# First load in one array, tiled head sums, ScalarE order and grouped state reads in a hybrid RWKV / attention / MoE block

## The chip, the cores and the metric

The kernel runs on one core of a Trainium2 chip. The metric is the device time of one execution in microseconds (us). The core has TensorE (PE in the profile), VectorE (DVE), ScalarE (ACT), GpSimd (POOL) and SyncE (SP, which here only issues DMAs). All arithmetic is float32.

## The reference

One layer on 256 tokens of width 1024: a combined input projection that feeds an RWKV7 group and a differential-attention group, an output projection, cross-attention to 256 memory tokens, and a mixture of 32 experts (top 4 per token). Cut to what matters here:

```python
xn = rms_norm(x, norm1_g); proj = xn @ w_in            # 1024 x 3328
p = p + (token_shift(p) - p) * mu                       # first 1792 columns
r, k, v, wd, ad, gd = split_cols(p, ...)                # r, k, v: 8 heads of 64
kk = (k * k_k).reshape(B, T, H, N)
kk = kk / maximum(sqrt(sum(kk * kk, -1)), 1e-12)        # one factor per head and token
def step(S, inp):                                       # recurrence over tokens
    sa = einsum('bhvk,bhk->bhv', S, -kkt)
    S = S * wt + sa * (kkt * at) + vt * kt
    return S, einsum('bhvk,bhk->bhv', S, rt)
h = x + concat([y_rwkv, y_diff]) @ w_out
h = h + cross_attn(rms_norm(h), rms_norm(mem))
h = h + moe(rms_norm(h))                                # 32 experts, 403 MB of weights
out = rms_norm(h, final_g)
```

## The kernel before

Everything is written out by hand in one function, `program` (L94), with one block per engine; the order in each block is the order in which that engine works, and semaphores are the only ties between them. PSUM has 8 banks. A table (`place`, from L277) gives each product a bank and a turn in it; `begin` makes TensorE wait until the bank's last user has been copied out ("drained"), `product` makes a reader wait until it is filled.

**Weights before the experts.** The projection weights are cut into chunks of 256 columns (1 MB each). SP loads them in the order of `PRE_CHUNKS` (L79) into a ring of three slots, a slot being free once the product that used it is finished. A chunk product on TensorE is 16 matmul calls (2 halves of 128 columns, 8 contraction steps, 256 tokens), each of which is two instructions of a profile row: 32 instructions a chunk. Chunks in2, in3, in6 are multiplied with x times the norm gain only (`gx`), and their products are scaled with the norm factors afterwards, by VectorE (`scale_products`, L1703); the factors come from TensorE (`factors`, L1001) out of a diagonal that VectorE computes from the sums of squares of x (`spread`, L1669). The other chunks use the normalised xT (L1711).

**The start.** SP issues x transposed and chunk in2 in three parts each, alternating (L474, L475), then x in rows (L478, for the sums of squares), then in3, mem, in6, mem transposed (L480 to L484) and small arrays. VectorE writes gx step by step (L1691), TensorE does the first half of in2 over its 8 steps, then the second.

**RWKV group.** ScalarE takes each product times 1 - mu (L704, `unshifted`), VectorE adds the shifted part (L1728, `shift`), which drains the bank. The head norm goes: kk squared (L1742), `ksum` on TensorE (L1033, four accumulating matmuls that sum each head's 64 rows into 8 rows), clamp and reciprocal root on VectorE (8 rows, L1762), `kb` on TensorE (L1059, which spreads the 8 rows back to 128), product on VectorE (L1786). Between ksum and kb stand chunk in1, the four groups of low-rank products (L1046, L1052; ScalarE drains them with L720 and L693) and chunk in4. The chain on VectorE from L1769 to L1810 gives AR and BT (`ab_ready`), from which TensorE forms L (L1079). The inverse of L's diagonal blocks goes out and in over small DMAs that ScalarE's queue issues (L745, L755, L761, L766), the last eight of them (L766) write XTb, which TensorE needs before chunk in11 (L1166). Then come the state matrices of 8 chunks of 32 tokens; `step(c)` (L1247) advances the state, VectorE adds (L1938), `read_state(c)` (L1262) reads it. Quarters of the chunk products kv2 and kv3 (`filler`) are put between the steps. VectorE also does `combine(2)` (L1878 to L1885) in that stretch, for which TensorE waits in `turn_weights(2)` (L995).

**The mem side.** ScalarE sums mem's squares (L679), VectorE makes the factors (L1667 to L1674), TensorE spreads them (L1008) and VectorE scales memT with them (L1682), all before chunk in0 and in1; memT is first used by kv0.

**Experts.** 96 units of 4 MB stream through five places in the chip's memory; a unit's load is issued when TensorE has finished with the one that held its place (L445, L511, L532). The first units are issued while w_out and wq_x are multiplied (L390 to L395).

## Time and profile before

| | us |
|---|---|
| runs of the kernel before: median of 3 (lowest to highest) | 1248.64 (1248.36 to 1252.04) |
| the profiled execution's own time | 1247.27 |
| its span in the profile | 1245.4 |
| PE busy in the span | 1198.3 (96%) |
| PE weight loads / DVE / ACT / POOL busy | 573.0 / 310.5 / 197.1 / 14.4 |
| chain that ended last | PE 71%, DMA 25%, ACT 2%, DVE 1%, issue 1% |
| HBM read | 443.47 MB, mean 357 GB/s |

TensorE's matmuls are pipelined, so a row's duration for one instruction (0.38 us for 256 columns) is longer than its share of a run of them (6.91 us for the 32 instructions of a chunk). The chain of work that ended last shows the second kind of number, which adds up; the timeline shows starts. A row's bracket says how long the engine was idle before it, and what ended that. "issue" is idle time that no semaphore of the profile explains. The granted TensorE clock was 1.00 of full speed in all stretches up to 1120 us and 0.99 in the rest. The first 338 us hold everything before the experts.

### The profile page before, as it was taken

The page shows a single profiled execution, that of the slowest core. Times are in us where ns is not written, and L with a number is a line of the kernel's source. Part 1 is how long each engine was busy: PE and PEld are TensorE (multiplying, and loading weights), DVE is VectorE, ACT ScalarE, POOL GpSimd, SP SyncE. Part 2 cuts the span into 40 slices and gives each one's busy share as a digit, 9 for nine tenths or more (in the row PEclk, how much of TensorE's full clock was granted, in tenths as well). Part 3 has the DMA queues.
Part 4 walks back from the last instruction along what each step waited for, and adds up shares of the span by engine and source line. Part 5 has one row for each costly group of instructions (what it writes and reads, how often), then busy time and mean ns, then how long its engine had stood idle before and what let it go on. Part 6 is the DMA issues. An engine that isn't in the chain of part 4 may idle for free.

```text
span 1245.4 us, 17482 instructions
## 1 busy us (share of the span) xinstructions
PE 1198.3 (96%) x7452; PEld 573.0 (46%) x7452; DVE 310.5 (25%) x771; ACT 197.1 (16%) x371; POOL 14.4 (1%) x56
## 2 busy tenths in 40 slices
PE   7998999999999999999999999989999999999998
PEld 6787878888733333333333333323333333333333
DVE  5774245203411211121121112111112211111212
ACT  2313243011211111111111111111111111111101
POOL 4000000000000000000000000000000000000000
PEclk9999999999999999999999999999999999999999
DMA  9332213937799999999999999999999999999995
GB/s 326 133 119 79 103 70 105 415 156 274 300 383 436 418 410 436 429 430 433 429 431 435 428 434 431 430 434 431 430 434 430 433 433 431 430 434 431 426 426 230
DMA packets 29922, 445.52 MB, mean 358 GB/s; under 512 B 8432, under 2 KB 8816, under 8 KB 11440
## 3 DMA queue, kind: packets, MB, share of 16 engines
q1 hardware_dynamic: 24944, 443.74, 84.8%
q10 hardware_dynamic: 4928, 1.05, 0.4%
q8 instruction: 39, 0.64, 0.2%
q14 instruction: 11, 0.09, 0.0%
HBM read 443.47 MB, written 1.31 MB: 357 GB/s over the span
## 4 chain that ended last, share of the span: by engine, by line
PE 71%; DMA 25%; ACT 2%; DVE 1%; issue 1%; ACTq 0%; SPq 0%; DVEq 0%
PE ps L1519 22%; DMA ring<-in_moe_w 15%; PE ps L1559 14%; PE ps L960 10%; DMA arena<-in_moe_w 9%; PE ps L981 7%; PE ps L1463 4%; PE ps L1437 3%; PE ps L1422 2%; PE ps L1451 1%; ACT arena L908 1%; PE ps L1168 1%; PE ps L1456 1%; PE ps L995 1%; DMA ring<-in_w_in 1%
## 5 line engine op out<-in xcount | busy, mean ns | idle before, releaser
L1519 PE MATMUL ps<-ring,arena 128*64 128x512 f32 x1248 | 273.6, 593 | 13.8 <-DMA ring<-in_moe_w 13.2
L1519 PE MATMUL ps<-arena 128*64 128x512 f32 x792 | 174.0, 593 | 8.5 <-DMA arena<-in_moe_w 8.5
L1519 PEld LDWEIGHTS ps<-ring,arena 128*64 128x64 f32 x1248 | 88.9, 137 | 194.2 <-issue 173.2
L1559 PE MATMUL ps<-ring,arena 128*64 128x512 f32 x576 | 127.7, 595 | 0.0
L900 ACT ACTIVATE arena<-arena 128x512 f32<-128x512 f32 x31 | 19.5, 629 | 678.8 <-DVE arena L2119 678.8
L2119 DVE TENSOR_SCALAR arena<-ps 128x512 f32<-128x512 f32 x31 | 21.4, 691 | 397.3 <-PE ps L1519 397.3
L960 PE MATMUL ps<-arena,ring 128*128 128x256 f32 x480 | 107.9, 385 | 8.0 <-DMA ring<-in_w_in 8.0
L1519 PEld LDWEIGHTS ps<-arena 128*64 128x64 f32 x792 | 56.4, 137 | 123.4 <-issue 109.6
L960 PEld LDWEIGHTS ps<-arena,ring 128*128 128x128 f32 x480 | 91.4, 192 | 22.0 <-issue 7.9
L1559 PE MATMUL ps<-arena 128*64 128x512 f32 x408 | 90.7, 595 | 0.4 <-DMA arena<-in_moe_w 0.4
L2132 DVE COPY arena<-ps 128x512 f32<-128x512 f32 x32 | 22.1, 692 | 234.9 <-PE ps L1559 234.9
L1559 PEld LDWEIGHTS ps<-ring,arena 128*64 128x64 f32 x576 | 39.8, 137 | 86.6 <-issue 86.6
L1463 PE MATMUL ps<-arena,rws 64*128 64x512 f32 x256 | 63.6, 615 | 0.2 <-DVE arena L2132 0.2
L1437 PE MATMUL ps<-arena 128*64 128x512 f32 x248 | 60.1, 605 | 0.0
L1559 PEld LDWEIGHTS ps<-arena 128*64 128x64 f32 x408 | 28.2, 137 | 61.6 <-issue 60.3
L2100 DVE TENSOR_TENSOR arena<-ps,prm 128x512 f32<-128x512 f32 x32 | 22.1, 691 | 87.7 <-PE ps L1451 85.5
L981 PE MATMUL ps<-ring,arena 128*128 128x256 f32 x192 | 42.6, 381 | 0.0
L1463 PEld LDWEIGHTS ps<-arena,rws 64*128 64x128 f32 x256 | 22.0, 186 | 40.7 <-issue 40.2
L693 ACT ACTIVATE arena<-ps 128x512 f32<-128x512 f32 (+1 forms) x39 | 21.9, 574 | 118.2 <-PE ps L960 52.3
L900 ACT ACT_TABLE_LOAD x31 | 39.8, 1283 | 1.3 <-issue 0.7
L981 PEld LDWEIGHTS ps<-ring,arena 128*128 128x128 f32 x192 | 36.2, 190 | 5.2 <-issue 0.4
L1422 PE MATMUL ps<-arena 32*64 32x512 f32 x264 | 35.9, 613 | 0.0
(308 smaller groups left out, 866.2 us busy)
## 6 DMA issues: line engine op xcount, KB each, us to landing
ring<-in_moe_w SPq DMA_DIRECT2D x51, 4096.0 KB, 35.2
arena<-in_moe_w SPq DMA_DIRECT2D x32, 4096.0 KB, 36.7
arena<-in_moe_w SPq DMA_DIRECT2D x12, 2048.0 KB, 27.3
ring<-in_moe_w SPq DMA_DIRECT2D x11, 2048.0 KB, 32.8
ring<-in_w_in SPq DMA_DIRECT2D x12, 1024.0 KB, 5.6
ring<-in_wkv_x SPq DMA_DIRECT2D x8, 1024.0 KB, 4.8
ring<-in_w_out SPq DMA_DIRECT2D x4, 1024.0 KB, 4.7
ring<-in_wq_x SPq DMA_DIRECT2D x4, 1024.0 KB, 7.2
```

The source lines that it names most:

```text
L693: drain(s.activation(dst, view(src) if view else src, ACT.Copy), name)
L900: s.activation(dst[:, :], src[:, :], ACT.Sigmoid, scale=1.702).then_inc(sem("sig_ready"), 1)
L960: ins = t.matmul(o[:, q * T:(q + 1) * T], w[:, k, q * P:(q + 1) * P], src[:, k, :], start=(k == 0), stop=(k == KC - 1))
L981: ins = t.matmul(o[:, i * WCOL:(i + 1) * WCOL], src[:, k, i * P:(i + 1) * P], w[:, k, :], start=(k == 0), stop=(k == KC - 1))
L1422: t.matmul(ps[c * BLK:(c + 1) * BLK, 4 + b, :], onehot[g, :], b1a[g, :], start=True, stop=False, tile_position=((2 * b + c) * E, c * BLK), ...
L1437: ins = t.matmul(ps[c * BLK:(c + 1) * BLK, 6, :], sel[:, i, :], h[:, i, c * 512:(c + 1) * 512], start=(i == 0), stop=(i == NT - 1), skip_g ...
L1463: t.matmul(ps[:, 2 * i + c, :], GT[rows, i * P:(i + 1) * P], yy[rows, :], start=False, stop=False, skip_group_check=True)
L1519: ins = t.matmul(ps[c * BLK:(c + 1) * BLK, 4 + b, :], xeT[:, col:col + BLK], w(k % 4)[:, f0:f0 + 512], start=False, stop=(k == KC - 1), sk ...
L1559: ins = t.matmul(ps[c * BLK:(c + 1) * BLK, 7, :], src[:, col:col + BLK], w(k // 2)[:, f0:f0 + 512], start=(k == 0), stop=(k == KC - 1), sk ...
L2100: v.tensor_tensor(xeT[:, :].rearrange("p (m c t) -> p m c t", m=4, c=2), ps[:, 6, :].rearrange("p (m c t) -> p m c t", m=4, c=2), gains, A ...
L2119: v.tensor_scalar(gg[:, :], ps[:, 4, :], 7.0, None, ALU.min).then_inc(sem("gate_ready"), 1)
L2132: v.tensor_copy(yy[:, :], ps[:, 7, :]).then_inc(sem("yy_ready"), 1)
```

## The change

- **First load.** x transposed and chunk in2 are put side by side in one input array, `first`, and loaded in five pieces of 1, 1, 2, 2 and 2 contraction steps, into a place of its own. TensorE does both halves of in2 in each step, in two banks (6 and 7). SP's order behind it is now in3, x in rows, in6, in0, the small arrays, in1, and then mem, mem transposed and the router's arrays. in0 no longer waits for a slot.
- **Order at the start.** Factors of x come after the whole of in3. mu1 and w0h are computed before x in rows is needed. The mem factors move back: sums of squares on ScalarE behind in7's copy, factors on VectorE after `ops_ready`, TensorE's part after in9, memT's scaling after `score_max(0)`, from a copy in the chip's memory.
- **Head sums.** ksum is four matmuls of 32 columns each, at column tiles 0, 32, 64, 96, without accumulation (each head pair has rows of its own among 128). kb is four matmuls of 32 rows, at row tiles 0 to 96, into four banks (2 to 5), and stands ahead of in4; it now waits for all four low-rank banks. VectorE's clamp and root run on 128 rows of 256 instead of 8.
- **Order on TensorE, VectorE and ScalarE.** L comes right after in5, ahead of in7. VectorE does shift(4) and the tail differences after `ab_ready`, and the update of k as one instruction. ScalarE takes in4 after two exponentials, in5 after the third, L ahead of in7, the second natural rows ahead of the eight XTb DMAs, and the MV copies ahead of `exps(0)`.
- **State reads.** The eight `read_state(c)` become two `read_states(i)` of four chunks, issued over eight tiles, the first ahead of step(4), the second at the end. `centre(0)` moves from c = 5 to 6.
- GpSimd zeroes XTb after `const_ready` instead of before it.

The diff, cut to its core:

```diff
+FIRST_PIECES = (slice(0, 1), slice(1, 2), slice(2, 4), slice(4, 6), slice(6, 8))
...
+        first = cut(AR0, KC, T + WCOL)
...
                 if n == 0:
-                    for m, (k0, k1) in enumerate(thirds):
-                        sp.dma_start(xT[:, k0:k1, :]..., a["x_turned"][:, k0 * T:k1 * T])...
-                        sp.dma_start(home(n)[:, k0 * WCOL:k1 * WCOL], a[w][part][:, k0 * WCOL:k1 * WCOL])...
-                    for i in range(NT):
-                        sp.dma_start(h[:, i, :], a["x"][0, i * P:(i + 1) * P, :])...
+                    for m, ks in enumerate(FIRST_PIECES):
+                        sp.dma_start(first[:, ks, :], a["first"][:, ks, :]).then_inc(sem(f"first{m}_in"), 16)
                     continue
...
+            for k in range(KC):
+                for m, ks in enumerate(FIRST_PIECES):
+                    if k == ks.start:
+                        pe.wait_ge(sem(f"first{m}_in"), 16)
                 pe.wait_ge(sem("gx_ready"), k + 1)
+                for q in range(2):
+                    ins = t.matmul(o[q][:, 0:T], w[:, k, q * P:(q + 1) * P], gx[:, k, :], start=(k == 0), stop=(k == KC - 1))
...
-                ins = t.matmul(o[0:NH, 0:T], hsel[:, j, :], t2[:, j, :], start=(j == 0), stop=(j == NP - 1))
+                ins = t.matmul(o[j * CH:(j + 1) * CH, 0:T], hsel[:, :, :].rearrange("p a b -> p (a b)"), t2[:, j, :], start=True, stop=True,
+                               tile_position=(0, j * CH))
...
+            pe.wait_ge(sem("knorm_ready"), 1)
+            o = [begin(pe, f"kb{j}") for j in range(NP)]
+            for j in range(NP):
+                rows = slice(j * CH, (j + 1) * CH)
+                done(t.matmul(o[j][:, 0:T], hselT[rows, :], krs[rows, :], start=True, stop=True, tile_position=(j * CH, 0)), f"kb{j}")
             turned("in4", xT)
...
+            def read_states(i):
+                o = [begin(pe, f"Y{i}{q}") for q in range(2)]
                 for j in range(NP):
+                    for c in range(P // CH):
+                        for q in range(2):
+                            rows = slice(q * HD, (q + 1) * HD)
+                            tok = slice(i * P + c * CH, i * P + (c + 1) * CH)
+                            ins = t.matmul(o[q][c * CH:(c + 1) * CH, j * HD:(j + 1) * HD], RhT[rows, j, tok], St[rows, 4 * i + c, j, :],
+                                           start=True, stop=True, tile_position=(q * HD, c * CH))
```

**TensorE, from ksum to L.** Before (L960 is a chunk, L1046 and L1052 the low-rank products):

```order
L1033 MATMUL ps<-arena,extra 8x256 x4
L960 MATMUL ps<-arena,ring 128x256 x16
L1046 MATMUL ps<-arena 128x256 x4
L1052 MATMUL ps<-arena 128x256 x2
L1046 MATMUL ps<-arena 128x256 x4
L1052 MATMUL ps<-arena 128x256 x2
L960 MATMUL ps<-arena,ring 128x256 x16
L1059 MATMUL ps<-arena,extra 128x256 x4
L960 MATMUL ps<-arena,ring 128x256 x32
L1079 MATMUL ps<-arena 32x32 x64
L960 MATMUL ps<-arena,ring 128x256 x16
```

and in the changed kernel, where L986 is a chunk, L1059 is ksum, L1085 kb, L1104 L, and L1021 the first turned rows:

```order
L1059 MATMUL ps<-arena,extra 32x256 x4
L986 MATMUL ps<-arena,ring 128x256 x16
L1073 MATMUL ps<-arena 128x256 x4
L1079 MATMUL ps<-arena 128x256 x2
L1073 MATMUL ps<-arena 128x256 x4
L1079 MATMUL ps<-arena 128x256 x2
L1085 MATMUL ps<-arena,extra 128x256 x4
L986 MATMUL ps<-arena,ring 128x256 x32
L1104 MATMUL ps<-arena 32x32 x64
L986 MATMUL ps<-arena,ring 128x256 x32
L1021 MATMUL ps<-ident,arena 128x128 x16
```

kb has moved ahead of in4, and L ahead of in7: three chunks stood between the low-rank products and L, now two do.

**ScalarE, from in10's copy to the first softmax.** Before (L693 is a copy out of PSUM, L766 the XTb DMAs, L779 the exponentials):

```order
L693 ACTIVATE arena<-ps 128x512 [waits bank0_filled]
L766 DMA ring<-blocks 16x16x16 [waits X_blocks_out]
L766 DMA ring<-blocks 16x16x16 x7
L693 ACTIVATE arena<-ps 128x8x64 [waits bank2_filled]
L693 ACTIVATE arena<-ps 128x512 [waits bank3_filled]
L798 ACTIVATE lam<-lam 128x2 [waits lam_sum_ready]
L779 ACTIVATE ring,extra<-ps,extra 128x128 [waits dmax_ready]
L779 ACTIVATE ring,extra<-ps,extra 128x128 [waits act_step] x3
L779 ACTIVATE ring,extra<-ps,extra 128x128 [waits bank2_drained]
L779 ACTIVATE ring,extra<-ps,extra 128x128 [waits act_step] x3
L693 ACTIVATE arena<-ps 128x8x64 [waits bank3_drained,bank6_filled,t3_free]
L693 ACTIVATE arena<-ps 128x8x64 [waits bank7_filled]
```

and now (copies L710, XTb DMAs L791, exponentials L803):

```order
L710 ACTIVATE arena<-ps 128x512 [waits bank0_filled]
L710 ACTIVATE arena<-ps 128x8x64 [waits bank2_filled]
L710 ACTIVATE arena<-ps 128x512 [waits bank3_filled]
L791 DMA ring<-blocks 16x16x16 [waits X_blocks_out]
L791 DMA ring<-blocks 16x16x16 x7
L822 ACTIVATE lam<-lam 128x2 [waits lam_sum_ready]
L710 ACTIVATE arena<-ps 128x8x64 [waits bank6_filled,t3_free]
L710 ACTIVATE arena<-ps 128x8x64 [waits bank7_filled]
L803 ACTIVATE ring,extra<-ps,extra 128x128 [waits dmax_ready]
L803 ACTIVATE ring,extra<-ps,extra 128x128 [waits act_step] x3
L803 ACTIVATE ring,extra<-ps,extra 128x128 [waits bank2_drained]
L803 ACTIVATE ring,extra<-ps,extra 128x128 [waits act_step] x3
```

The two copies of banks 2 and 3 (natural rows) have moved ahead of the eight DMAs, and those of banks 6 and 7 (MV) ahead of the exponentials.

**TensorE, around the states.** Before (L1247 is a step, L1262 a state read, L960 a quarter of a chunk, L995 `turn_weights(2)`, L1139 `values(2)`):

```order
L1247 MATMUL ps<-arena,ring 64x64 x8
L960 MATMUL ps<-ring 128x256 x4
L1262 MATMUL ps<-arena 32x64 x16
L1247 MATMUL ps<-arena,ring 64x64 x8
L960 MATMUL ps<-ring 128x256 x4
L1262 MATMUL ps<-arena 32x64 x8
L1247 MATMUL ps<-arena,ring 64x64 x8
L995 MATMUL ps<-ident,ring 128x128 x4
L960 MATMUL ps<-ring 128x256 x4
L1262 MATMUL ps<-arena 32x64 x8
L1247 MATMUL ps<-arena,ring 64x64 x8
L1139 MATMUL ps<-arena 128x128 x4
```

and now (step L1274, state reads L1286, quarter L986, `turn_weights(2)` L1021, `values(2)` L1166):

```order
L1274 MATMUL ps<-arena,ring 64x64 x8
L986 MATMUL ps<-ring 128x256 x4
L1274 MATMUL ps<-arena,ring 64x64 x8
L986 MATMUL ps<-ring 128x256 x4
L1274 MATMUL ps<-arena,ring 64x64 x8
L1021 MATMUL ps<-ident,ring 128x128 x4
L986 MATMUL ps<-ring 128x256 x4
L1286 MATMUL ps<-arena 32x64 x32
L1274 MATMUL ps<-arena,ring 64x64 x8
L1166 MATMUL ps<-arena 128x128 x4
L986 MATMUL ps<-ring 128x256 x4
L1274 MATMUL ps<-arena,ring 64x64 x8
```

Between step(2) and `turn_weights(2)` no state read stands any more, nor ahead of step(2); the first 32 calls come together after `turn_weights(2)`.

## Rows read from the trace of the kernel before

**Rows 1.** Busy time by stretch (start:end, PE, PEld, DVE, ACT, POOL, PEclk, DMA share, GB/s).

```profile
101.90:116.00 14.10, 10.48 (x184) 8.02 (x185) 6.01 (x17) 6.14 (x22) 0.00 (x0) 1.00 0.33 86
...
338.00:1245.40 907.40, 875.95 (x4188) 297.33 (x4188) 168.01 (x374) 112.64 (x165) 0.00 (x0) 1.00 0.98 420
```

**Rows 2.** TensorE's waits up to 280 us (total, times, longest).

```profile
PE ps L960 <- DMA ring<-in_w_in: 8.0, 2, 7.1
PE ps L1168 <- ACT arena L693: 1.8, 1, 1.8
PE ps L1125 <- ACT arena L693: 1.3, 1, 1.3
```

**Rows 3.** SP's waits before it issues loads of expert units.

```profile
SPq L445 <- PE ps L1519: 394.6, 57, 8.4
```

**Rows 4.** Timeline of the start (start, duration, engine, line).

```profile
7.12 3.75 PE L960 MATMUL ps<-arena,ring 128*128 128x256 f32 x8 [7.12 <-DMA ring<-in_w_in]
...
11.74 4.55 PE L960 MATMUL ps<-arena,ring 128*128 128x256 f32 x20 [0.88 <-DMA ring<-in_w_in]
...
14.20 1.23 DVE L1693 SCALAR_TENSOR_TENSOR arena<-arena 128x1024 f32<-128x1024 f32 x1 [3.16 <-DMA arena<-in_x]
```

**Rows 5.** Timeline of VectorE before chunk in0.

```profile
24.69 0.69 DVE L1706 TENSOR_TENSOR ps<-ps,arena 128x512 f32<-128x512 f32 x1
...
27.90 0.48 DVE L1674 TENSOR_SCALAR arena<-ident,st 128x128 f32<-128x128 f32 x2
...
29.52 1.00 DVE L1728 SCALAR_TENSOR_TENSOR arena<-ps,prm,arena 128x255 f32<-128x255 f32 x2 [0.23 <-DVE arena L1728]
```

**Rows 6.** Chain that ended last, 11 to 60 us (start, us, what).

```profile
11.74 8.87 PE ps L960 x40
...
31.87 6.91 PE ps L960 x32
38.77 1.82 PE ps L1033 x8
40.60 7.11 PE ps L960 x32
47.70 1.06 PE ps L1046 x8
...
58.86 1.92 PE ps L1059 x8
```

**Rows 7.** Timeline of ScalarE and VectorE from the low-rank products to L.

```profile
51.03 1.85 ACT L720 ACTIVATE arena<-ps,w0h 128x256 f32<-128x256 f32 x4
...
52.12 0.69 DVE L1769 TENSOR_SCALAR arena<-arena 128x1024 f32<-128x1024 f32 x1 [2.42 <-ACT arena L720]
...
72.48 1.23 DVE L1810 TENSOR_TENSOR arena<-arena 128x1024 f32<-128x1024 f32 x1
```

**Rows 8.** Timeline: 64 calls over eight tiles of 64 rows by 32 columns.

```profile
84.79 1.48 PE L1099 MATMUL ps<-arena 64*32 64x64 f32 x128
```

**Rows 9.** Timeline of TensorE, from the scores to z1.

```profile
107.37 1.16 PE L1125 MATMUL ps<-arena 64*128 64x128 f32 x16 [1.34 <-ACT arena L693]
...
110.39 3.72 PE L981 MATMUL ps<-ring,arena 128*128 128x256 f32 x16
...
115.96 3.69 PE L1168 MATMUL ps<-arena,ring 32*32 32x128 f32 x128 [1.85 <-ACT arena L693]
```

**Rows 10.** The XTb DMAs by their line (duration ns, first and last start, landing).

```profile
L766 ACTq DMA_DIRECT2D ring<-blocks x8: 347/470/657, 101.9 to 105.4; - x8
...
DMA to landing us min/median/max: 3.6/4.4/5.4
```

**Rows 11.** DMA queues from 104 to 105 us (packets, MB, share).

```profile
q1 hardware_dynamic: 49, 0.40, 96.3%
q10 hardware_dynamic: 44, 0.00, 2.9%
```

**Rows 12.** Chain that ended last, state reads of one and of two chunks.

```profile
182.49 0.57 PE ps L1262 x16
...
188.69 0.83 PE ps L1262 x32
```

**Rows 13.** Timeline: `turn_weights(2)` behind `combine(2)`.

```profile
176.10 0.42 PEld L995 LDWEIGHTS ps<-ident,ring 128*128 128x128 f32 x4 [0.28 <-DVEq L1887]
```

More of the change, by code:

```diff
@@ L277, in program @@
         place("x_factors", 2)
-        chunk("in2")
+        for q in range(2):
+            place(f"in2{q}", 6 + q)
+        where["in2"] = where["in20"]
         chunk("in3")
-        place("mem_factors", 3)
         chunk("in6", 4)
@@ L747, in _ @@
                    .then_inc(sem("L_blocks_out"), 16)
+            copy(qd[:, 0:2, :], "in7", two)
+            act.wait_ge(sem("mem_in"), 16)
+            for i in range(NT):
+                link(s.activation(mem_squares[:, :], memN[:, i, :], ACT.Square, accum_out=st[:, i:i + 1]))
+            act.sem_inc(sem("stat_ready"), 1)
             def natural_rows(i):
@@ L1108, in _ @@
             turned("in9", xT)
+            factors("mem", mdiag)
             chunk_products(1)
@@ L1270, in _ @@
                 taken(pe, f"Rh{c}")
[L1271 to L1279 removed]
+            pe.wait_ge(sem("S_ready"), 4)
+            read_states(0)
             step(4)
@@ L1731, in shift @@
                         link(ins)
-                dlink(ins, f"in{m}")
+                if m == 2:
+                    link(ins)
+                    for q in range(2):
+                        dve.sem_inc(drained[where[f"in2{q}"][0]], 1)
+                else:
+                    dlink(ins, f"in{m}")
                 dve.sem_inc(sem("shifted_ready"), 1)
@@ L1811, in _ @@
             dve.sem_inc(sem("ab_ready"), 1)
+            shift(4)
+            product(dve, "lg1")
+            for j in range(NP):
+                ins = v.tensor_tensor(t34[:, j], tail[:, j, :].unsqueeze(2).to_broadcast([P, NCH, CH]), cs4[:, j], ALU.subtract)
+            link(ins)
+            dve.sem_inc(sem("rest_ready"), 1)
             shift(5)
+            link(v.scalar_tensor_tensor(out=kT[:, :, :], in0=KT[:, :, :], scalar=1.0, in1=kT[:, :, :], op0=ALU.add, op1=ALU.mult))
             link(v.tensor_tensor(KT[:, :, :], kT[:, :, :], t1[:, :, :], ALU.mult))
```

196 lines of the change are left out of this document (88 added, 108 removed).

## Prediction, made before the changed kernel ran

> **What bounds the kernel now.** Read first the busy time by stretch. From 338 us on the DMA engines are busy for 0.98 of the time at 420 GB/s, while TensorE is busy 875.95 us of 907.40 [rows 1]: the expert stage ends with its stream of weights. Read next whom SP waits for: its loads of expert units wait for TensorE, 57 times and 394.6 us in all [rows 3]. So the stream is paced by releases at its start and by its own rate afterwards, and a shift of everything before 338 us should move the end by as much. In that first part TensorE has the work: it waited there 8.0 us for the first weights, 1.8 us and 1.3 us for ScalarE [rows 2]. What the change is worth is therefore what it takes from TensorE's queue before the experts, plus the waits that it removes, less the waits that it makes. Faster or slower by over 0.3% (3.7 us) is about what a measurement of this kernel can tell from no change.
>
> All positions below are in the span of the profiled execution. Its own time is 1247.27 us; the median of the runs shown is 1248.64, 1.37 above.
>
> **The start.** Before, TensorE starts at 7.12, does four calls, stands still for 0.88 and resumes at 11.74 for the 12 calls that in2 still needs [rows 4]. From there 20 calls take 8.87 [rows 6], 0.44 a call, so in2 ends at 17.1. Now both halves of a step follow its piece. The bytes to be landed before step 2 are those of before, and so I take the same start at 7.12; 16 calls at 0.432 (6.91 for 16 [rows 6]) are 6.9, and a gap of some 0.2 for the third piece makes 14.2: a gain of 2.8. The last piece lands with the 2nd MB, as the last part did at 11.7 [rows 4], and after it only four calls (1.7) are to do, so it doesn't end last. in3's weights are now the 3rd MB, which was x's last half before, landed at 14.2 (VectorE starts on it at 14.20 [rows 4]): in step with TensorE, to a few tenths. Bounds: 2.9 without a gap, 1.6 if each landing is a microsecond late.
>
> x's last half now lands behind in3, one MB later, at 16.7 if 1 MB takes 2.5 us at the 420 GB/s of rows 1. Square, root and diagonals took from 14.2 to about 18.4 (4.2), so they are ready at 20.9, and TensorE wants them after in3, at 21.1. From the factors VectorE has 7.2 us of work to the end of shift(3), which drains in3's bank: the mem factors' 2.9 (from 25.4 to 28.4 [rows 5]) leave the interval that ended at 30.5 [rows 5]. That is 28.3, and TensorE, done with in6 at 28.6, begins in0 there instead of at 31.87 [rows 6]. The 0.44 for the mem factors come back behind in9, so the start is worth 2.8. Its cover is 0.3 us thin: what delays x delays in0.
>
> **ksum.** 1.82 us for four full calls, one after the other [rows 6]. No row shows four tiles of 128 rows by 32 columns. The nearest rows: the low-rank calls, two row tiles at once, put four calls of 256 columns into 1.06 [rows 6]; and 128 instructions over eight tiles, four of them beside each other in columns, take 1.48 [rows 8], 0.0116 each where 64 columns alone need 0.054 (a quarter of a chunk instruction's 0.216). So column tiles do run side by side. I take one call (0.43) plus 0.2 for the change of tiles, which the chunk after ksum shows (7.11 against 6.91 [rows 6]): 0.65, a gain of 1.2. Bounds: 0.5 and 1.82. The Trainium skill (TensorE: Matmul & The Clock Gate, measured speedup of packing) has 2.38 times for three column tiles and 3.07 for four row tiles; by 3.07 ksum would be an estimated 0.59, which no run here has shown yet.
>
> **kb and its new wait.** The four low-rank groups take 4 times 1.06, from 47.70 to 51.95 [rows 6]. ScalarE's last tanh ends at 52.88 [rows 7]; kb needs its bank, and kb now stands right there: TensorE waits 0.95, with in4 and everything else queued behind it. Before, in4 covered this. kb itself goes from 1.92 [rows 6] to 0.65 by the same reasoning. Net gain 0.3; bounds from 1.3 (no wait) to a loss of 0.95 (wait, and tiles one after the other).
>
> **L ahead of in7.** VectorE's chain from 52.12 to 73.71 [rows 7] loses the wait for kb (2.2), shift(4) and the tail differences (2.9) and half of k's update (1.8), and ends 19.1 after in1's end, where it ended 26.0 after. TensorE reaches L at 4.25 + 0.95 + 0.65 + 13.9 = 19.8 after in1. L should not wait, with 0.7 to spare. VectorE is then late with natural rows by about 1 us, before in10, where TensorE has some 8 us of chunk work as cover. memT's scaling (8 instructions, 3.2 us) goes beside ScalarE's exponentials, which take 4.0: it costs nothing unless these shorten.
>
> **The ScalarE order.** Between 101.90 and 116.00 TensorE idles 3.6 of 14.1 us [rows 1]. 1.34 of it is the natural rows behind the eight DMA issues, 1.85 the MV copies behind the exponentials [rows 9]. Both go. What is late next: XTb. Its last DMA was issued at 105.4 and landed at most 3.6 later, at 109.0 [rows 10], 1.4 before TensorE wanted it for in11 at 110.39 [rows 9]. Now the issues start two copies (1.15) later and TensorE arrives 1.34 earlier: 109.0 + 1.15 against 109.05, a wait of 1.1, if the landing takes as long. The eight stood behind kv0's weights: while these flowed, both queues moved about packet for packet (49 against 44 in a microsecond [rows 11]), and XTb's packets are tiny. kv0's load is issued at the same place as before, so the later DMAs find it done sooner, and I take a wait of 0.3. Gain 2.9, bounds 2.1 and 3.2. The Trainium skill (DMA: Bandwidth & Descriptors, queues, rings and completion order) says that an engine takes turns between queues at packet granularity; rows 11 agree, and by that rule the wait would be near zero, by the landing time of rows 10 alone 1.1.
>
> **State reads.** 0.57 for one chunk, 0.83 for two [rows 12], in four single and two double places: 3.94. Two groups of 32 calls each, spread over the same kind of eight tiles as the 64 calls of rows 8, cost 0.7 + 0.15 each, 1.7 in all: a gain of 2.2. But a read (0.57) stood between step(2) and `turn_weights(2)`, and TensorE already waited there 0.2 for `combine(2)` [rows 13], which hangs on step(2) alone: 0.57 of the gain is a new wait. `centre(0)` one step later lies beside filler. Net 1.65; bounds 0 (the tiles gain no more than two at once) and 2.2.
>
> **Sum.** 2.8 + 1.2 + 0.3 + 2.9 + 1.65 = 8.85 us. From 1247.27 that gives 1238.4, and against the median of the runs 1239.8, which I forecast. With the small ends of all bounds it is a gain of 2.8 and with the large ones 10.8; terms this independent seldom fall on the same side, so 4.5 to 10.8 stands for the forecast and its near neighbours.
>
> **Rivals.**
> - *Late x and late XTb* (0.16). For: the covers are 0.3 and 0 us. If x's half lands 1 us later and XTb takes its 3.6, 0.7 + 0.8 go, and kb's wait grows nothing: 7.3; with another 1 us at in3's weights 6.3, so 1241 to 1242.
> - *The full-height column tiles don't overlap* (0.06). ksum keeps 1.82, kb keeps its 1.7 and its wait (0.95 - 0.2), and the reads gain only their changes of tile. Left: 2.8 + 2.9 - 0.75 = 4.95, so 1243.7. Against it speaks rows 8.
> - *The end doesn't follow the start* (0.06). If the stream of weights were bound to its rate from the first unit on, its end would move less than TensorE's beginning; with a third of the shift passed on, 3 us, 1245.7. Against: SP's waits [rows 3].
> - *Slower: the stream runs at a lower rate* (0.04). Its place is the expert stage: 907 us at 420 GB/s [rows 1], so each per cent of rate is worth 9.1 us, a mean below 416 GB/s undoes the whole gain, and below 414 it would be slower by over 3.7 us: 1252.4. The change moves no expert load against another, which is why the chance is small.
> - The forecast itself has 0.68.
>
> **How the numbers follow.** Faster by over 3.7 us: forecast, late x, and most of the tiles' case, 0.88. Within: 0.08, the third rival and the weak end of the second. Slower 0.04. The range from 1237 to 1244.2 takes in the forecast's bounds and the first two rivals.
>
> **What would show it.** In the changed profile: in2's first call near 7.1 and in3's end near 21; in0 at 28.6; ksum's eight instructions within 0.7 us; a TensorE wait of about 0.95 for ScalarE ahead of kb, L without a wait at 63; in10's end near 97.6; no waits for ScalarE before the scores and z1, one of 0 to 1.1 for XTb ahead of in11; 0.7 us for `combine(2)`; reads of 0.85 each; the expert stage unchanged in length and rate. The prediction is wrong if in0 starts after 30, if L waits for VectorE by over 1 us (then the order on VectorE, not the tiles, sets the middle), or if the first expert matmul comes 8 us earlier and the end doesn't.

## Result, and the profile after the change

| | before | changed |
|---|---|---|
| first comparison: median (lowest to highest) | 1248.64 (1247.42 to 1252.05), 5 runs | 1240.86 (1240.27 to 1243.00), 5 runs |
| the same pair compared a second time (e9) | 1248.72 (1247.01 to 1254.36), 11 runs | 1240.39 (1239.50 to 1242.39), 6 runs |
| profiled execution: own time, span | 1247.27, 1245.4 | 1242.53, 1240.7 |

The ratio is 0.9938 (95% interval 0.9918 to 0.9958), and 0.9928 (0.9912 to 0.9944) in the second comparison: 7.8 and 8.3 us faster. The forecast was 1239.8 with a range of 1237.0 to 1244.2, so the time lies 1.1 us above the forecast and inside the range.

TensorE's positions in the two traces (start of the first instruction in the timeline, us) say where the time came from. z1 is the product behind chunk in11. The last column has the terms of the prediction's sum, with the 0.44 of the mem factors counted where they stood and where they now stand.

| place | before | changed | gained since the line above | predicted |
|---|---|---|---|---|
| in0 | 31.70 | 29.01 | 2.69 | 3.24 (2.8 + 0.44) |
| in1 (behind ksum) | 40.53 | 36.66 | 1.18 | 1.2 |
| second natural rows (behind kb, L, in10) | 101.73 | 98.17 | -0.31 | -0.14 (0.3 - 0.44) |
| z1 | 115.96 | 110.06 | 2.34 | 2.9 |
| kv4 (behind the state reads) | 193.01 | 185.62 | 1.49 | 1.65 |
| first expert product | 338.22 | 331.86 | -1.03 | 0 |
| end of the span | 1245.44 | 1240.71 | -1.63 | 0 |

Up to kv4 the gain is 7.4, against 8.85 predicted. (The chain of [rows 6] has in0 at 31.87 and in1 at 40.60: where two instructions overlap it starts the second only at the end of the first, 0.17 and 0.07 later here.) The last two lines are no work of the change; they are taken up with e9.

The chain that ended last in the changed kernel, from 5 to 50 us (start, us, what), answers to [rows 6]:

```profile
5.24 9.24 PE ps L1047 x32
14.49 6.91 PE ps L986 x32
...
23.19 2.29 DVE arena L1724
...
28.38 0.49 DVE arena L1739
...
29.01 7.14 PE ps L986 x32
36.16 0.57 PE ps L1059 x8
36.73 7.10 PE ps L986 x32
...
48.53 0.48 ACT arena L737
...
49.15 0.71 PE ps L1085 x8
```

in2 is L1047. Its 32 instructions take 9.24 us where a whole chunk takes 6.91, and they start at 5.24, not at 7.12 [rows 4]. Behind in3 the chain leaves TensorE for VectorE: the scaling of xT, then shift(3), and in0 starts 0.13 after that. ksum is 0.57 for 1.82, kb 0.71 for 1.92. Ahead of kb the chain passes through ScalarE's last tanh.

The waits of TensorE up to 280 us (total, times, longest), against [rows 2]:

```profile
PE ps L1274 <- issue: 1.1, 1, 1.1
PE ps L1085 <- ACT arena L737: 1.1, 1, 1.1
PE ps L1007 <- DMA ring<-blocks: 0.9, 1, 0.9
PE ps L1253 <- issue: 0.8, 1, 0.8
PE ps L1021 <- DVEq L1902: 0.7, 1, 0.7
```

The two waits for ScalarE of before (1.34 and 1.85) are gone. Besides the 0.3 at in0 there are three new ones, all foreseen as places: kb's (0.95 predicted, 1.1 found), XTb's ahead of in11 (0.3 predicted, with 1.1 as the bound; 0.9 found), `combine(2)`'s (0.7 and 0.7). The "issue" rows were there before too, with 1.01 and 0.54.

How XTb came late, from the chain at 98 us on (L791 issues the eight DMAs, L710 is a copy):

```profile
98.37 1.09 ACT arena L710 x2
99.46 0.12 ACTq L791
...
102.10 1.10 ACTq L791
...
103.23 3.14 DMA ring<-blocks
...
106.41 3.72 PE ps L1007 x16
```

The last of the eight issues began at 103.23, and its 16 KB landed 3.14 us after that; the last of before had taken 3.6, the shortest of [rows 10]. The issue ahead of it took 1.10 us, where the others took 0.47. All eight, and kv0's 1 MB (L497), by their lines (duration ns, first and last start, us to landing):

```profile
L791 ACTq DMA_DIRECT2D ring<-blocks x8: 325/470/1101, 99.2 to 103.2; - x8
DMA to landing us min/median/max: 2.8/3.5/4.5
...
L497 SPq DMA_DIRECT2D ring<-in_wkv_x x1: 328/328/328, 98.4 to 98.4; - x1
DMA to landing us min/median/max: 5.3/5.3/5.3
```

The issue of 1.10 began at 102.10 and landed the quickest, after 2.8 us, so seven of the eight loads were there at 104.9, and TensorE was ready for in11 at 105.5: it waited for the eighth alone. The order of landing tells more. kv0's weights landed at 103.7, and the first XTb load, issued at 99.25, just behind them at 103.8, the next six 0.2 apart; in the kernel before it was 107.3 and 107.4. In both traces the small loads issued beside the large one landed only behind it, whatever turns the packets took [rows 11].

### The profile page after: what moved, and what is told of

It is laid out like the page before. It is cut to its first block, busy times and chain, and to the rows that moved or that the text cites. A ratio compares the mean times of both kernels' runs of the same rounds, so it can differ in the third digit from the quotient of the medians.

```text
span 1240.7 us, 17494 instructions
## 1 busy us (share of the span) xinstructions
PE 1195.3 (96%) x7452; PEld 570.6 (46%) x7452; DVE 309.7 (25%) x768; ACT 197.8 (16%) x372; POOL 14.7 (1%) x59
## 4 chain that ended last, share of the span: by engine, by line
PE 71%; DMA 25%; ACT 2%; DVE 1%; issue 1%; ACTq 0%; DVEq 0%; SPq 0%
PE ps L1540 22%; DMA ring<-in_moe_w 15%; PE ps L1580 14%; PE ps L986 10%; DMA arena<-in_moe_w 9%; PE ps L1007 7%; PE ps L1484 4%; PE ps L1458 4%; PE ps L1443 2%; PE ps L1472 1%; ACT arena L932 1%; PE ps L1195 1%; PE ps L1047 1%; PE ps L1477 1%; PE ps L1021 1%
## 5 line engine op out<-in xcount | busy, mean ns | idle before, releaser
L1540 PEld LDWEIGHTS ps<-ring,arena 128*64 128x64 f32 x1248 | 88.9, 137 | 194.2 <-issue 172.9
L986 PE MATMUL ps<-arena,ring 128*128 128x256 f32 x448 | 98.8, 380 | 0.3 <-DVE arena L1739 0.3
L986 PEld LDWEIGHTS ps<-arena,ring 128*128 128x128 f32 x448 | 84.5, 190 | 12.8 <-issue 1.4
L1007 PE MATMUL ps<-ring,arena 128*128 128x256 f32 x192 | 42.6, 381 | 0.9 <-DMA ring<-blocks 0.9
L710 ACT ACTIVATE arena<-ps 128x512 f32<-128x512 f32 (+1 forms) x39 | 21.9, 574 | 113.1 <-PE ps L986 51.0
L1007 PEld LDWEIGHTS ps<-ring,arena 128*128 128x128 f32 x192 | 36.2, 190 | 6.2 <-DMA ring<-blocks 1.1
```

What stands on the lines that cost most here:

```text
L710: drain(s.activation(dst, view(src) if view else src, ACT.Copy), name)
L986: ins = t.matmul(o[:, q * T:(q + 1) * T], w[:, k, q * P:(q + 1) * P], src[:, k, :], start=(k == 0), stop=(k == KC - 1))
L1007: ins = t.matmul(o[:, i * WCOL:(i + 1) * WCOL], src[:, k, i * P:(i + 1) * P], w[:, k, :], start=(k == 0), stop=(k == KC - 1))
L1540: ins = t.matmul(ps[c * BLK:(c + 1) * BLK, 4 + b, :], xeT[:, col:col + BLK], w(k % 4)[:, f0:f0 + 512], start=False, stop=(k == KC - 1), sk ...
```

## Experiments

Each is an edit of the changed kernel, and each position is read in the trace of its own run. Where positions are compared between runs, the difference is taken from in0's start on, since the start itself differs by up to 1 us between runs that begin in the same way (below, e4). e1 to e8 ran once each (1240.56 to 1244.54 us, e5 1262.45), which is too little to tell half a microsecond by the whole time.

**e1. kb in banks that the last tanh does not hold.**

```
-            place(f"kb{j}", 2 + j)
-        chunk("in4")
-        for n in (5, 7, 8, 9, 10):
+            place(f"kb{j}", (2, 3, 0, 1)[j])
+        chunk("in4", 4)
+        chunk("in5", 5)
+        for n in (7, 8, 9, 10):
```

> Edit of the changed kernel: kb's third and fourth product go to banks 0 and 1 in place of 4 and 5, so that kb needs no bank of the last tanh; in4 and in5 move to banks 4 and 5. In the changed kernel TensorE waited 1.1 us at kb for ScalarE's last tanh; L started at 63.88 without a wait, VectorE having finished the operands of L at 63.36. Theory: the wait is one for la1's bank alone. Then kb waits 0 to 0.2 us, in4 begins at 48.9 instead of 49.86, but L gains only half of it: TensorE arrives at 62.9 and waits about 0.5 for VectorE, whose chain starts from the tanh and not from kb. L starts at 63.4 and the first z1 product 0.5 earlier than 110.1. Rival: kb waits for ScalarE's arithmetic and not for a bank, or the chain on VectorE moves along; then L starts at 63.9 or at 62.9.

**e2. kb behind in4 again, L left ahead of in7** (the five lines of kb moved below `turned("in4", xT)`).

> Edit of the changed kernel: the four kb products move from ahead of in4 to behind it, where the kernel before had them; L keeps its place ahead of in7. Theory: the 1.1 us of wait at kb go, but kb ends at about 48.05 + 7.1 + 0.7 = 55.9, 1.9 later than VectorE came for it (53.96), so L's operands are ready at 65.3 and TensorE, there at 62.9, waits 2.4: L starts 1.4 later than in the changed kernel (63.9). Rival: VectorE has slack and L starts at 62.9, so that the wait that the change made was a plain loss of 1.1.

Timeline of TensorE, first e1 (in0, kb, L), then e2 (in0, L):

```profile
29.74 7.14 PE L987 MATMUL ps<-arena,ring 128*128 128x256 f32 x32 [0.26 <-DVE arena L1740]
...
49.07 0.71 PE L1086 MATMUL ps<-arena,extra 32*128 32x256 f32 x8 [0.27 <-issue]
...
64.20 1.29 PE L1105 MATMUL ps<-arena 64*32 64x32 f32 x128 [0.41 <-DVEq L1818]
```

```profile
29.74 7.14 PE L986 MATMUL ps<-arena,ring 128*128 128x256 f32 x32 [0.26 <-DVE arena L1739]
...
65.99 1.55 PE L1104 MATMUL ps<-arena 64*32 64x32 f32 x128 [2.53 <-DVEq L1817]
```

In the changed kernel L comes 34.8 us after in0 (29.01 to 63.80). In e1 it is 34.5: kb's wait is 0.27, and 0.41 of what that frees is waited for at L; z1 comes 80.6 after in0 in place of 81.1. In e2 it is 36.25, 1.45 later, with a wait of 2.53 for VectorE (and z1 2.6 later, as the clock fell in the course of that wait). Both are as the theory had them. kb ahead of in4, wait and all, was the right side of the choice: L's operands hang on kb, with 0.5 us to spare.

**e3. The XTb loads ahead of three copies on ScalarE.**

```
+            act.wait_ge(sem("X_blocks_out"), 16)
+            for j in range(P // SUB):
+                ...
             copy(kd[:, 2:4, :], "in10", two)
             natural_rows(1)
-            act.wait_ge(sem("X_blocks_out"), 16)
-            for j in range(P // SUB):
-                ...
```

> Edit of the changed kernel: ScalarE issues the eight XTb loads ahead of its copies for in10 and the second natural rows, not behind them. In the changed kernel TensorE waited 0.92 us for them at in11. X's blocks were stored with an issue at 93.93 that took 1.8 to land, so the eight issues run from about 96 to 100.3 and land by 104.8. Theory: the wait of 0.92 at in11 goes, in11 starts at 105.5; the three copies, now from 100.3 to 102, still come before the scores at 102.4. z1 at 109.2 instead of 110.1. Rival: the copies come late and TensorE waits for ScalarE at the natural rows or scores (0.5 or more), or the landing of the last takes longer beside kv0's weights and the wait stays.

```profile
105.81 3.72 PE L1007 MATMUL ps<-ring,arena 128*128 128x256 f32 x16
109.46 1.07 PE L1195 MATMUL ps<-arena,ring 32*32 32x128 f32 x32
110.74 1.51 PE L1195 MATMUL ps<-arena,ring 32*32 32x128 f32 x48 [0.20 <-ACT ring L803]
```

in11 (L1007) starts without a wait and z1 comes 80.1 after in0, 81.1 in the changed kernel. Inside z1 a new wait of 0.2 for an exponential takes a part back: z1 lasts 4.0 in place of 3.6, so 0.6 is left behind it. With it the term "the ScalarE order" would have had all of its 2.9: what it lacked was the place of these eight issues. Here the six that were issued ahead of kv0's load landed after 1.8 to 2.2 us. The two issued with it and just behind it (98.75, 99.25) took 4.9 and 4.8 and landed, once more, right behind its weights.

**e4. Constants multiplied ahead of in2.**

```
+            for _ in range(7):
+                t.matmul(ps[:, 5, 0:P], ones[:, :], ones[:, :], start=True, stop=True)
             w = weights("in2")
```

> Edit of the changed kernel: seven calls on constants (128 columns each) from about 1.9 us on, ahead of in2, into an unused bank; they compute nothing that is used. In the changed kernel TensorE's first ten instructions, from 5.24 to 9.5, took 0.427 each (the 1.2 GHz level) and those behind 0.216 (2.4 GHz). Theory: the level rises a few us after the engine has begun to work, so it rises at about 6.2; in2 is then paced by its pieces (the last at 10.24) and ends at 12.3 instead of 14.5, in3 waits for its weights until 12.8 and ends at 19.8, and in0 starts at 27.3 instead of 29.0, since VectorE's chain of 7 us hangs on the factors, which stand behind in3. Rival 1: the level rises at a fixed time after the start of the program, 9.5, whatever the engine does: no gain. Rival 2: the gaps between the pieces keep the level down, in2 ends at 13 or later. Rival 3: x's own chain (15.4 to 19.5) holds the factors, and in0 stays at 28.5 or later.

First, the question behind it. TensorE's instructions of in2 up to 9.4 us in the changed kernel (ns: shortest, median, longest; first and last start), and all 32 of them:

```profile
L1047 PE MATMUL ps<-arena x10: 524/631/763, 5.2 to 9.2; 128*128 128x256 f32 x10
...
L1047 PE MATMUL ps<-arena x32: 379/379/763, 5.2 to 14.1; 128*128 128x256 f32 x32
```

Ten instructions start 0.427 apart, those from 9.5 on 0.216 apart: the 1.2 GHz level and the 2.4 GHz level. (The column of the granted clock says 1.00 there only because it has no entry ahead of its first, which is the rise. For the same reason the 1.00 told for all stretches of the kernel before holds only from 11 us on.) The kernel before did this too: its first eight, from 7.12, are 0.427 apart; those from 11.74 on are 0.216 apart. [Rows 4] show it as 3.75 us for eight instructions beside 4.55 for twenty. In eleven profiled runs that begin with in2 the rise came between 3.4 and 6.1 us after the engine's first instruction, and so the start of in3 varies: 14.2 to 15.2 us with five pieces. With the work on constants, e4:

```profile
1.94 3.35 PE L1040 MATMUL ps<-ones 128*128 128x128 f32 x14 [1.94 <-POOL ones L631]
5.08 8.33 PE L1049 MATMUL ps<-arena 128*128 128x256 f32 x32
13.25 7.07 PE L986 MATMUL ps<-arena,ring 128*128 128x256 f32 x32
...
27.93 7.14 PE L986 MATMUL ps<-arena,ring 128*128 128x256 f32 x32 [0.26 <-DVE arena L1741]
...
161.88 0.26 PE L1255 MATMUL ps<-arena 32*64 32x64 f32 x1 [1.86 <-issue]
162.07 2.08 PE L1168 MATMUL ps<-arena 128*128 128x128 f32 x8
```

The rise came at 7.6, in3 started at 13.25 (14.32 in the same view of the changed kernel) and in0 at 27.93: 1.1 gained, 1.7 expected (the rise was expected at 6.2, and TensorE, not the pieces, still set in2's end). Rival 1 falls: the level follows the work. The Trainium skill (TensorE: Matmul & The Clock Gate, The HAM clock gate) says that the clock rises after the engine has been busy for a while and that the number of slow instructions differs from run to run; the traces agree, with 8 to 14 of them in those eleven runs.

The whole run was slower than its neighbours, though (1244.54): at 161 us there is an issue time of 1.86, and behind it a product that took 1.16 elsewhere took 2.08. Granted clock (the figure ahead of the last two) in e4:

```profile
160.00:165.00 5.00, 3.14 (x27) 2.71 (x24) 0.88 (x3) 3.97 (x13) 0.00 (x0) 0.62 0.00 0
```

**e5. The price of tiles by itself** (64 calls of 256 columns ahead of ksum, into unused banks).

```
+            for _ in range(4):
+                for j in range(NP):
+                    t.matmul(ps[j * CH:(j + 1) * CH, 5, 0:T], ..., t2[:, j, :], start=True, stop=True, tile_position=(0, j * CH))
...
+                    t.matmul(ps[0:CH, 5, 0:T], ..., t2[:, j, :], start=True, stop=True, tile_position=(0, 0))
...
+                    t.matmul(ps[:, (2, 3, 5, 7)[j], 0:T], hselT[rows, :], t2[rows, 0, :], start=True, stop=True, tile_position=(j * CH, 0))
...
+                    t.matmul(ps[:, 6, 0:T], hselT[0:CH, :], t2[0:CH, 0, :], start=True, stop=True, tile_position=(0, 0))
```

> Edit of the changed kernel: 64 calls of 256 columns are added ahead of ksum, into unused banks, four kinds of 16: head sums on four tiles of 128 rows by 32 columns in turn; the same with all on the first such tile; head factors on four tiles of 32 rows by 128 columns in turn; the same with all on the first such tile. Theory: what makes ksum (0.57 for four calls) and kb (0.71) short is that calls on different tiles run beside each other. Then 16 calls take about 1.9 to 2.3 us in turn and 6.9 on one tile (0.43 each), for both kinds. Rival: a call is cheap because it writes only 32 columns or reads only 32 rows; then the calls on one tile are as fast as those in turn.

```profile
36.41 1.93 PE L1059 MATMUL ps<-arena,extra 128*32 128x256 f32 x32
38.17 7.07 PE L1063 MATMUL ps<-arena,extra 128*32 128x256 f32 x32
45.17 2.01 PE L1068 MATMUL ps<-arena,extra 32*128 32x256 f32 x32
47.00 9.33 PE L1071 MATMUL ps<-arena,extra 32*128 32x256 f32 x31
```

From start to start: 1.76 us for 16 calls over four column tiles and 7.0 on one, 4.0 times; 1.83 over four row tiles, and 0.43 a call on one while the clock held. So the gain is overlap between tiles, and neither the 32 columns nor the 32 rows are cheap in themselves. In the last group the clock fell, to a mean of 0.51 from 51 to 61 us; the engine had worked without a pause up to there, from 47 us on with one tile of 32 by 128.

**e6. The state reads as they were before.** The piece of the order between `step(1)` and kv4, and `read_state`, are taken from the kernel before; `centre(0)` goes back by one step.

> Edit of the changed kernel: the state reads are put back as before the change, one or two chunks at a time between the steps. In the changed kernel kv4's first call came 79.2 us after in11's (106.41 to 185.62), with 0.79 for each group of four chunks, a wait of 0.73 for VectorE at turn_weights(2) and 1.9 of issue time at two small products. Theory: 3.94 for the reads in place of 1.58, and the 0.73 shrink to 0.2: kv4 comes 81.0 us after in11, 1.8 later. Rival 1: the reads were partly hidden before (they overlap the steps around them), so the difference is under 1. Rival 2: nothing shrinks, 81.6.

in11 starts at 106.23 and kv4 at 186.41 (80.2), the issue time between them is 0.55 + 0.57. In the changed kernel these are 79.2 and 1.9. So the plain difference is 1.0, as rival 1 had it; at equal issue time the old reads are 1.77 longer. e1 has the new reads and the issue time of e6 (1.1), and needs 78.4, 1.8 less: the term of 1.65 is confirmed, and both rivals fall.

**e7. Exponentials ahead of the MV copies again** (`exps(0)` moved above the two copies).

> Edit of the changed kernel: ScalarE takes the exponentials ahead of the two MV copies again. In the changed kernel the first z1 product started at 110.13 without a wait and the exponentials ran from 106.31 to 110.2. Theory: the copies come from 110.2 to 111.8 and TensorE waits for them, z1 starts at 111.8, 1.6 to 1.7 later, the difference that the order is worth now (before, 1.85). Rival: the copies are no longer needed at that time, or the loads of XTb end later than 106.4, and the difference is under 0.5.

```profile
106.62 3.72 PE L1007 MATMUL ps<-ring,arena 128*128 128x256 f32 x16 [1.13 <-DMA ring<-blocks]
111.05 2.17 PE L1195 MATMUL ps<-arena,ring 32*32 32x128 f32 x72 [0.70 <-ACT arena L710]
```

z1 comes at 111.05, 1.0 later, of which the wait for ScalarE is 0.7, not 1.6. Two things were overlooked. z1 can begin with the first of the two copies (110.39 + 0.6), and the wait for XTb just ahead covers a part: where in11 was on time, the same order had cost 1.85 [rows 9].

**e8. Three pieces in place of five.**

```
-FIRST_PIECES = (slice(0, 1), slice(1, 2), slice(2, 4), slice(4, 6), slice(6, 8))
+FIRST_PIECES = (slice(0, 2), slice(2, 4), slice(4, 8))
```

> Edit of the changed kernel: the joint array of x and in2 comes in three pieces (2, 2 and 4 steps) in place of five (1, 1, 2, 2, 2). Theory: TensorE's first call moves from 5.2 to about 5.9, its lower level of clock therefore ends 0.7 later, and the last piece lands at 10.2 with eight calls behind it in place of four; in2 ends 0.7 to 1.5 later than in the changed kernel and its neighbours (14.5 to 15.1), and in0 as much later than 29.0 to 29.7. Rival: the last piece alone sets the end of in2; then in2 ends at most 0.3 later. Rival 2: x's chain sets in0, and in0 doesn't move.

```profile
6.69 9.58 PE L1047 MATMUL ps<-arena 128*128 128x256 f32 x32 [6.69 <-DVE arena L1704]
16.11 7.07 PE L986 MATMUL ps<-arena,ring 128*128 128x256 f32 x32
```

The first call comes 1.45 later and in2 ends 1.8 later, in0 at 30.79, a little more than expected (beside the other runs with five pieces in3 starts 0.9 to 1.9 later). In neither kernel does TensorE stand still inside in2, so it is not the large last piece that delays it: in2 ends later because it begins later and has two more instructions at the lower level (12, not 10). So about half or more of what the start gained is owed to the small first piece: TensorE begins its slow instructions earlier. What it is worth to do both halves in each step no run shows by itself.

**e9 to e12. The changed kernel again, and three versions of it, on one chip.** e10 puts together e1, e3, in0 in bank 3 and the following; e11 and e12 add work on constants.

```
+            link(v.tensor_tensor(Bd[:, :, :], kk[:, :, :], aa[:, :, :], ALU.mult))
-            for j in range(NP):
-                link(v.tensor_scalar(KT[:, j, :], aa[:, j, :], 1.0, pr("k_a", j), ALU.subtract, ALU.mult))
-            link(v.tensor_tensor(aa[:, :, :], kk[:, :, :], aa[:, :, :], ALU.mult))
...
             dve.sem_inc(sem("ab_ready"), 1)
+            for j in range(NP):
+                link(v.tensor_scalar(KT[:, j, :], aa[:, j, :], 1.0, pr("k_a", j), ALU.subtract, ALU.mult))
...
+            for _ in range(2):
+                t.matmul(ps[:, 5, :].rearrange("p (a b) -> p a b", a=4), ones[:, :],
+                         ones[:, :].unsqueeze(1).to_broadcast([P, 4, P]), start=True, stop=True)
```

> The changed kernel unaltered, so that the next three can be set against it on one chip. Its times there were 1240.3 to 1243.0, median 1240.86. In its profile the clock fell to its lower level for 3.4 us at 323.5, which no other profile but one shows at that place; theory: a run without such a fall takes 1240.3 to 1241, and one with it 1 to 2 us more, so the median is 1240.5 to 1241.5 and the first expert call comes at 330.5 where the clock holds.

> The changed kernel with four small edits: kb's last two products in banks 0 and 1 (e1), VectorE's k update moved behind the operands of L by way of another buffer (1.5 us of VectorE), the XTb loads ahead of the copies (e3), and in0 in bank 3, so that it need not wait for in3's bank. Theory: kb's wait 1.1 goes to 0.3 and L does not wait (e1 gained 0.5 alone, now 0.8 to 1.0), the XTb wait 0.9 goes (0.7 net, as an exponential is late by 0.2), in0 gains 0.26: kv4's first call is 1.8 to 2.2 us nearer to in2's end than in the changed kernel at equal issue time, and the median is 1.8 to 2.2 below that of e9. Rival: what TensorE gains is waited for at the first place where VectorE or ScalarE is the later one, and less than 1 arrives at the end.

> As e10, with two calls of 512 columns on constants ahead of in2, into an unused bank (4 instructions in the place of the 14 of e4). Theory: in2 ends at 13 to 13.5 as in e4 (13.25), where the others had 14.2 to 15.1, and the end follows: 1 to 1.8 below e10. The fall of the clock at 161 in e4 belongs to the issue time there, 1.86 ahead of one instruction, and that to where the stream of instructions is cut, so with few instructions added it should not come. Rival: the fall comes from the early rise itself and is seen again, and the gain is lost (within 0.5 of e10).

> As e11, but with the seven calls of e4 (14 instructions). Theory: the issue time of e4 (0.94 at 105.3, 0.75 at 157.7 and 1.86 at 160, against 1.1 in all in most others) comes back in these places because the same number of instructions stands ahead, and with it in some or all runs the lower clock for 3.4 to 6.8 us: 1 to 4 us slower than e11. Rival: e4's stall was chance; then e12 is within 0.5 of e11.

| | median (lowest to highest), 6 runs | ratio to before (95%) | from in3's start to kv4, issue time in it |
|---|---|---|---|
| before | 1248.72 (1247.01 to 1254.36), 11 runs | | |
| e9 | 1240.39 (1239.50 to 1242.39) | 0.9928 (0.9912 to 0.9944) | 171.2, 1.65 |
| e10 | 1239.20 (1237.87 to 1245.21) | 0.9927 (0.9905 to 0.9949) | 169.2, 1.94 |
| e11 | 1237.30 (1236.82 to 1238.63) | 0.9907 (0.9891 to 0.9923) | 169.4, 2.38 |
| e12 | 1241.64 (1238.18 to 1244.14) | 0.9939 (0.9919 to 0.9959) | 172.9, 4.29 |

e10 gains the 2.0 us up to kv4 that were expected, but only 1.2 in the median, and the ranges of its runs and of e9's overlap: where the rest went is not shown. e11 is the best version, 11.4 us below before and 3.1 below the changed kernel; all six of its runs lie below all six of e9. Its start and its middle:

```profile
1.94 3.78 PE L1041 MATMUL ps<-ones 128*128 128x512 f32 x4 [1.94 <-POOL ones L632]
5.52 7.91 PE L1050 MATMUL ps<-arena 128*128 128x256 f32 x32
13.27 7.07 PE L987 MATMUL ps<-arena,ring 128*128 128x256 f32 x32
...
20.62 13.98 PE L987 MATMUL ps<-arena,ring 128*128 128x256 f32 x64
...
156.62 1.53 PE L1256 MATMUL ps<-arena 32*64 32x64 f32 x119 [1.07 <-issue]
```

in6 and in0 are now one unbroken row of 64, since in0 needs no bank of shift(3). That wait was printed as 0.26, but without it in1 comes 21.83 after in3 (e10, e11, e12) and with it 22.33 (all the others with five or three pieces but e5): 0.5. A bracket counts from the end of the instruction before, with which the next would otherwise have overlapped. e12 differs from e11 only in its 14 narrow instructions in the place of 4 wide ones, and is 4.3 us slower in the median, a little more than the 1 to 4 expected:

```profile
104.27 0.27 PE L1187 MATMUL ps<-arena,ring 32*32 32x64 f32 x2 [0.87 <-issue]
...
157.62 1.60 PE L1256 MATMUL ps<-arena 32*64 32x64 f32 x128 [1.03 <-issue]
161.35 0.26 PE L1256 MATMUL ps<-arena 32*64 32x64 f32 x1 [2.13 <-issue]
161.54 2.08 PE L1169 MATMUL ps<-arena 128*128 128x128 f32 x8
```

These are the places of e4 to the instruction (two left over at 104, one at 161).
**The last two lines of the first table.** In e9's profile the changed kernel had again a stretch at the lower level, as in its first profile. Granted clock of the stretch 323 to 329 us, the changed kernel and e3:

```profile
323.00:329.00 6.00, 6.00 (x38) 3.42 (x38) 3.70 (x24) 2.69 (x6) 0.00 (x0) 0.72 0.96 411
```

```profile
323.00:329.00 6.00, 5.67 (x50) 4.42 (x48) 2.84 (x20) 2.57 (x6) 0.00 (x0) 1.00 0.90 380
```

It costs about 1.0 us: from kv4 to the first expert product it is 146.2 with it (changed kernel, e9, e10) and 145.2 without (before, e3, e11, e12). The profiled run of e9 took 1242.39, the other five 1239.5 to 1240.7, with a mean clock of 0.999 in place of 0.998. So both profiled runs of the changed kernel are 1.7 to 2 us above its medians, and the profiled run of before was 1.4 below its own: together that is the difference between the 4.7 of the spans and the 7.8 and 8.3 of the medians. From the first expert product to the end of the span the runs took 907.2 (before, e11) to 909.6 (e3) whatever stood ahead of it, a scatter of 2.4 with no order in it by start. Over first products from 327.91 to 338.22 the end followed the start within that scatter.

## Why the prediction was right, and where its steps failed

**What bounds the kernel.** Right. The gain came from the part ahead of the experts, and the end followed it. The third rival (a third of the shift arrives) would have given 2.5 of the 7.4 us at the end; the medians show 7.8 and 8.3. The slower rival does not show: 420 GB/s [rows 1] are still 420.

**The start: 2.8 predicted, 2.4 found by the prediction's own measure (in0 at 29.01, not 28.6), by luck: two errors nearly cancel.** The step that failed is "I take the same start at 7.12", with the reason that as many bytes land ahead of step 2 as before. What TensorE waits for first is step 0, and the first piece holds half of the bytes that it had waited for; it started at 5.24. The other is the term "16 calls at 0.432": the first five ran at the lower level of the clock, 0.85 each, which costs 2.1, and that price stood in [rows 4], as 0.47 us an instruction for the first eight. Together they put in2's end at 14.49, 0.3 behind the 14.2 predicted. The rest is the cover that the text called 0.3 thin: in0 waited 0.27 for shift(3), and that cost 0.5 at in1, as e10 shows. e8 (in0 at 30.79 with a larger first piece) and e4 (27.93 with an earlier rise) show the two parts apart.

**ksum and kb.** Right in kind and nearly in size: 0.57 and 0.71 for 0.65 each. By own starts ksum took 1.83 and takes 0.57, a gain of 1.26, of which 0.08 goes into a longer in0. The chain's row of in0 (7.14, was 6.91) is longer mainly because in0 now starts behind a wait. The Trainium skill (TensorE: Matmul & The Clock Gate, Part 3, measured speedup) has 3.07 times for four row tiles with 512 columns; e5, with 256 columns, measures 3.8 for four of them (against the 0.43 a call on one tile before the clock fell) and 4.0 for four column tiles, so here the measurement decides: the overlap is nearly whole. kb's net was 0.1 and not 0.3, since its wait was 1.1 and not 0.95.

**L ahead of in7.** Right: no wait, 0.5 us of cover where 0.7 was worked out. e2 shows what the cover is worth.

**The ScalarE order: 2.9 predicted, 2.3 found, within its bounds of 2.1 to 3.2.** The failed step is "the later DMAs find it done sooner, and I take a wait of 0.3". XTb's wait was 0.9, beside the 1.1 of the landing time of [rows 10]. A wait of 0.3 asked for a landing 2.8 us after the last issue; it took 3.14, and an issue of 1.10 put its start 0.2 later than the shifts of the prediction give. In each of the nine runs with this order one of the last three issues took 0.85 to 1.10, and in e3 and e10 to e12 none over 0.48; why is open. Behind the step stands the reading that both queues move packet for packet and so the small loads get through: they landed behind kv0's weights. The first rival had named this case. The fix was not a faster landing beside the large load but an issue ahead of it (e3).

**State reads: 1.65 predicted, 1.49 found,** 1.77 in e6 at equal issue time. The reads are 0.79 each and `combine(2)` takes 0.73 back, as said.

**The sum.** 8.85 against 7.4, by own starts: 0.55 at the start, nothing at ksum, 0.2 at kb, 0.6 at XTb, 0.2 at the reads. "Terms this independent seldom fall on the same side", and four of five did, the fifth on neither, since most had been taken nearer to their good end than to the bad one. The medians, with 7.8 and 8.3, stand between the two; that the forecast is only 1.1 off in the median and 1.5 off up to kv4 is in part the luck of the start.

## What to carry to other kernels

Price the first instructions of a program at the lower clock, and give TensorE something to multiply as soon as anything is there; but do it in few, wide instructions. Where a table of instructions is long, as here, the count ahead of a burst of small ones is itself a quantity of the design. When a change removes waits for one engine, look for the small transfer that now ends last, and issue it before the copies that do not feed it and before the large load. A head sum or a spread over heads cost about a third with its four calls on four tiles (0.57 for 1.82, 0.71 for 1.92), and a quarter in the longer rows of e5. A wait can cost more than its bracket says (0.5 for 0.26 at in0, 0.4 for 0.2 inside z1 in e3).

## What the runs showed of the hardware that was not expected

- The lower level at the start lasts from 3.4 to 6.1 us after TensorE's first instruction, differently in each run of one program; it moves in2's end by up to 1 us (14.2 to 15.2).
- Stalls with no semaphore stand in bursts of small products: 1.1 to 1.9 us in all around the same few products (150 to 170 us, in e5 182 to 186) in eleven profiles, 2.1 in e11, and 2.6 and 3.2 in e4 and e12, which have ten instructions more than e11 ahead of them and one more stall at 104 to 105. The two that stand in all profiles are 127 or 128 matmul instructions apart.
- The clock fell to its lower level in the midst of work, for 3.4 to 10.2 us: in the longest stall of e4 and of e12, in the course of a wait of 2.5 us at L in e2 (0.71 from 64 to 68 us), during calls on one small tile in e5, and at 322 to 324 us in four profiles (changed kernel, e7, e9, e10). For the last, TensorE was busy for 4.53 of the 5 us from 318 on both where it fell and in e3, where it did not. Why it falls in some runs is open.
- Four tiles side by side gave 4.0 times in columns and 3.8 in rows, with 256 columns of f32.
- Eight small loads (16 KB each) issued beside a load of 1 MB landed 2.8 to 5.4 us after their issue, the first of them right behind the 1 MB (before, changed kernel); ahead of it six of them took 1.8 to 2.2 (e3).
